# A mended order of seven products, one quarter read straight from its bank, and a re-dealt start and end around it, in a hybrid decoder layer

## The reference, cut to what matters

```python
h = rmsnorm(x, ln_pre)
z = h @ w_in        # columns: c_val, c_glu, c_gate, q, k, v, a_gate, g_conv, g_attn
u = c_val * sigmoid(c_glu)
c = causal_depthwise_conv(u, w_dw, taps=31) + b_dw
ya = (silu(layernorm(c)) @ w_pw * silu(c_gate)) @ w_br_conv
yb = (sliding_window_attention(rope(q), rope(k), v) * silu(a_gate)) @ w_br_attn
m = sigmoid(g_conv) * ya + sigmoid(g_attn) * yb
x = x + rmsnorm(m @ w_out, ln_post)
x = x + sigmoid(x @ w_ple_gate) * (p @ w_ple_proj)
```

## Time and profile before

| | us |
|---|---|
| median of 3 runs | 1156.72 (1155.39 to 1156.76) |
| the profiled execution | 1154.67 |
| its span | 1152.9 |
| PE busy, share of the span | 1109.1, 96% |
| DVE busy | 946.6, 82% |
| ACT, POOL busy | 482.8 (42%), 316.3 (27%) |
| granted clock of PE, mean | 0.988 |

### The profile page before, as it was taken

One profiled execution on the slowest core, in us unless ns is written; L12 is line 12 of the kernel. 1 busy time (PEld: TensorE's weight loads), 2 busy tenths in 40 slices (PEclk: granted clock), 3 DMA queues, 4 the chain that ended last, 5 costly groups with the idle time before them and its releaser, 6 DMA issues.

```text
span 1152.9 us, 16104 instructions
## 1 busy us (share of the span) xinstructions
PE 1109.1 (96%) x6040; PEld 898.0 (78%) x6040; DVE 946.6 (82%) x1092; ACT 482.8 (42%) x909; POOL 316.3 (27%) x218
## 2 busy tenths in 40 slices
PE   9799999999999949989999999999999999999998
PEld 8677777777777838867777788888888888888887
DVE  6998989989999996989888589769767968557776
ACT  6524343343433211157666443332536435444332
POOL 2067778787865941520000000000000000000000
PEclk9999999999999979999999999999999999999999
DMA  9802131221314213277871211236454653334555
GB/s 351 318 0 73 37 140 43 76 107 37 110 40 161 74 42 69 52 191 212 214 199 57 73 37 55 78 126 225 149 167 133 231 208 112 125 119 139 178 202 182
DMA packets 49540, 148.21 MB, mean 129 GB/s; under 512 B 5536, under 2 KB 6304, under 8 KB 47424
## 3 DMA queue, kind: packets, MB, share of 16 engines
q1 hardware_dynamic: 35648, 92.77, 23.9%
q10 hardware_dynamic: 11520, 37.75, 9.3%
q0 software_dynamic: 2304, 16.78, 6.0%
HBM read 119.37 MB, written 41.94 MB: 140 GB/s over the span
## 4 chain that ended last, share of the span: by engine, by line
PE 83%; DVE 8%; DMA 3%; ACT 2%; POOL 1%; issue 1%; SPq 1%; DVEq 0%; ACTq 0%; POOLq 0%
PE psg L740 35%; PE psg L927 23%; PE psb L1170 10%; PE psg L1078 6%; DVE last_sums L2037 3%; PE psb L992 1%; PE psg L1049 1%; PE psg L1170 1%; DMA conv<-xT 1%; DMA x_rows<-x_rows 1%; PE psg L793 1%; PE psg L1123 1%; PE psg L1010 1%; ACT kept L1434 1%; PE psg L1044 1%
## 5 line engine op out<-in xcount | busy, mean ns | idle before, releaser
L2037 DVE SCALAR_TENSOR_TENSOR psb<-conv,cols,psb 128x1021 f32<-128x1021 f32 (+6 forms) x196 | 232.9, 1265 | 0.0
L927 PE MATMUL psg<-early_hi,pair_w 128*128 128x512 f32 x448 | 139.4, 392 | 10.9 <-ACT kept L1434 10.9
L1229 POOL TENSOR_TENSOR pair_w<-early_raw,pair_w 128x512 fp32r<-128x512 f32 x91 | 125.2, 1381 | 62.0 <-ACT pair_w L1422 61.7
L740 PE MATMUL psg<-h_hi,w_hi 128*128 128x512 f32 x320 | 101.0, 397 | 23.5 <-POOL w_lo L1222 23.5
L927 PEld LDWEIGHTS psg<-early_hi,pair_w 128*128 128x128 f32 x448 | 83.0, 188 | 33.1 <-POOL pair_w L1229 15.2
L1212 POOL TENSOR_TENSOR rstd<-mean_sq,expo 128x4 f32<-128x4 f32 x3 | 3.1, 1021 | 381.0 <-DVE mean_sq L1874 363.4
L927 PE MATMUL psg<-h_hi,pair_w 128*128 128x512 f32 x336 | 103.5, 389 | 0.0
L1860 DVE TENSOR_TENSOR w_lo<-w_raw,w_hi 128x1024 fp32r<-128x1024 f32 x55 | 67.3, 1224 | 41.1 <-ACT w_hi L1335 40.8
L740 PE MATMUL psg<-h_hi,w_lo 128*128 128x512 f32 x320 | 99.5, 392 | 0.0
L740 PE MATMUL psg<-h_lo,w_hi 128*128 128x512 f32 x320 | 99.4, 392 | 0.0
L740 PEld LDWEIGHTS psg<-h_hi,w_hi 128*128 128x128 f32 x320 | 60.6, 191 | 37.5 <-issue 17.2
(11 more groups left out here) (338 smaller groups left out, 2598.7 us busy)
## 6 DMA issues: line engine op xcount, KB each, us to landing
w_raw<-weights SPq DMA_DIRECT2D x68, 512.0 KB, 3.4
gates<-ring ACTq DMA_DIRECT2D x24, 512.0 KB, 3.6
w_sums<-w_pairs POOLq DMA_DIRECT2D x12, 1024.0 KB, 7.8
ring<-gates ACTq DMA_DIRECT2D x24, 512.0 KB, 4.4
block_raw<-w_sums SPq DMA_DIRECT2D x32, 256.0 KB, 3.0
early_raw<-w_pairs SPq DMA_DIRECT2D x7, 1024.0 KB, 5.3
block_raw<-w_pairs SPq DMA_DIRECT2D x24, 256.0 KB, 3.6
early_raw<-w_pairs SPq DMA_DIRECT2D x7, 768.0 KB, 4.3
```

The lines of the kernel that those rows point to most:

```text
L740: mm = nc.tensor.matmul(psg[:, slot, h * HALF:(h + 1) * HALF], w[:, wslot, (wk + k) * P:(wk + k + 1) * P], r[:, k, h * HALF:(h + 1) * HALF ...
L927: mm = nc.tensor.matmul(bank, pair_w[:, at_w, w, k * P:(k + 1) * P], r[:, k, :], start=(not onto and k == 0 and m == 0), stop=(k == KP - 1 ...
L1229: nc.gpsimd.tensor_tensor(pair_w[:, at_w, 1, :], early_source(s, n), pair_w[:, at_w, 0, :].bitcast(F32), ALU.subtract).then_inc(early_spli ...
L2037: own.step(stt(dst, row[:, 0:S - shift], tap(shift), dst, ALU.mult, ALU.add))
```

## The change

The order of the seven products becomes P1, Q5, P6, P2, P7, Q3, P4. Quarter 1 is taken by DVE as kept Q5 minus P7's bank, so ACT's copy of P7 goes away, and P4 waits for that DVE operation. Around it: at the start the low halves of tiles 2 and 3 go from POOL to DVE and ACT's and DVE's operations there are re-ordered, `plain_input(0)` writes to `sums` and not to `conv`; the last part of the convolution uses PSUM like the others; DVE does two taps and not eleven before the stages and one more in each odd stage that is not VAL; after the stages ACT takes the sines after q tile 0, POOL does `low(Q0 + 2)` before it waits for them, and one `add_to_mean` moves back.

```diff
-ORDER = (P1, P2, Q5, P6, P7, Q3, P4)
+ORDER = (P1, Q5, P6, P2, P7, Q3, P4)
...
-            if q == KT - 1:
-                return last_sums[n][:]
             return psb[:, 2 * n:2 * n + 2, :].rearrange("p b s -> p (b s)")
...
-                if onto:
-                    pe.wait_ge(early_kept, kept_at(s, {P6: P1, P7: P6, Q3: Q5, P4: P7}[n]))
+                if n == P4:
+                    pe.wait_ge(early_read, early_read_by(s, 1))
+                elif onto:
+                    pe.wait_ge(early_kept, kept_at(s, {P6: P1, P7: P6, Q3: Q5}[n]))
...
-                    pe.wait_ge(conv_done, KT - 1)
+                    pe.wait_ge(conv_done, KT)
...
# POOL
-            nc.gpsimd.memset(sums[:], 0.0).then_inc(csum_done, 1)
...
             low(1)
-            low(2)
-            low(3)
             for s in range(len(EARLY)):
                 early_low(s, P1)
                 early_sum(s, Q5)
-                early_low(s, P2)
                 early_sum(s, P7)
                 early_low(s, Q5)
                 early_sum(s, P6)
+                early_low(s, P6)
+                early_low(s, P2)
                 early_sum(s, P4)
-                early_low(s, P6)
                 early_low(s, P7)
                 early_low(s, Q3)
                 early_low(s, P4)
+                if s == 3:
+                    pool.wait_ge(conv_done, 1)
+                    nc.gpsimd.memset(sums[:], 0.0).then_inc(csum_done, 1)
...
-            add_to_mean(4)
+            low(Q0 + 2)
             pool.wait_ge(sin_ready, 1)
...
-            for t in range(Q0 + 2, C0 - 1):
+            for t in range(Q0 + 3, C0 - 1):
                 low(t)
-            add_to_mean(5)
+                if t in (Q0 + 3, Q0 + 4):
+                    add_to_mean(t - Q0 + 1)
...
# ACT
+            high(0, 2)
+            product_done(0, 0)
+            nc.scalar.activation(tanh_t[:], psg[:, 0, :], ACT.Tanh, scale=0.5).then_inc(ps_free[0], 1)
             early_sum_high(1, 1)
+            high(0, 3)
             early_sum_high(2, 2)
-            product_done(0, 0)
-            high(0, 2)
-            nc.scalar.activation(tanh_t[:], psg[:, 0, :], ACT.Tanh, scale=0.5).then_inc(ps_free[0], 1)
-            high(0, 3)
             early_sum_high(0, 3)
...
-                if n in (P1, Q5, P6, P7):
+                if n in (P1, Q5, P6):
                     early_keep(s, n)
...
-                if j == 1:
+                if j == 0:
                     act.wait_ge(ang_ready, 1)
...
# DVE
+            early_row_sum(1, 0)
+            dve.wait_ge(w_lo_ready, PLE_STEPS + 2)
+            tile_low(2)
+            early_row_sum(2, 1)
+            early_row_sum(0, 2)
+            plain_input(0)
+            early_row_sum(3, 3)
+            tile_low(3)
             dve.wait_ge(tile_done, KT)
...
-                    a, b, op = ((early_bank(s, P2), kept[:, 0, :], ALU.add), (kept_q5[:], kept[:, 0, :], ALU.subtract),
+                    a, b, op = ((early_bank(s, P2), kept[:, 0, :], ALU.add), (kept_q5[:], early_bank(s, P7), ALU.subtract),
...
-            plain_input(0)
-            taps(11)
+            taps(2)
             plain_input(1)
             for s, (kind, i) in enumerate(EARLY):
                 for n in ORDER:
-                    if n == Q5:
-                        dve.wait_ge(early_made, 7 * s + PLACE[Q5] + 1)
+                    if n == P2:
                         early_take(s, 0)
+                    if n == P7:
+                        early_take(s, 1)
                     if n == Q3:
-                        early_take(s, 1)
                         early_take(s, 2)
                     if n == P4 and kind == VAL:
                         early_take(s, 3)
-                    if n == Q5:
+                    if n == P2:
                         taps(1 if kind == VAL else 2)
                     elif n == Q3:
-                        taps(0 if kind == VAL else 1)
+                        taps(0 if kind == VAL else 1 + s % 2)
                     else:
                         taps(2)
...
-            taps(26)
+            taps(TAPS * KT)
```

More of the change, by code:

```diff
@@ L156, in build @@
         early_rest = at("early_rest", [HALF], F32, GB + 14 * KB)
-        last_sums = [at(f"last_sums{n}", [S], F32, GB + KB * (28 + 4 * n) - 192) for n in range(2)]
         v_last = at("v_last", [P], F32, GB + 24 * KB - 192)
@@ L540, in kept_at @@
         def kept_at(s, n):
-            return 4 * s + {P1: 1, Q5: 2, P6: 3, P7: 4}[n]
+            return 3 * s + {P1: 1, Q5: 2, P6: 3}[n]
         def early_read_by(s, n):
@@ L1428, in early_keep @@
                     act.wait_ge(ps_free[1], K_TILE // 2 + 4)
[L1429 to L1430 removed]
                 elif s > 0:
[L1432 to L1433 removed]
+                    act.wait_ge(early_read, early_read_by(s - 1, {P1: 0, Q5: 1, P6: 2}[n]))
+                dst = {P1: kept[:, 0, :], P6: kept[:, 1, :], Q5: kept_q5[:]}[n]
                 nc.scalar.activation(dst, early_bank(s, n), ACT.Copy).then_inc(early_kept, 1)
@@ L1997, in early_row_low, with plain_input @@
                 nc.vector.tensor_tensor(early_lo[:, n], sum_of(n), early_hi[:, n].bitcast(F32), ALU.subtract).then_inc(early_s_ready, 1)
-            for made, n in enumerate((1, 2, 0, 3)):
-                early_row_sum(n, made)
+            def plain_input(q):
+                product_done(q, 1)
+                dve.wait_ge(ps_free[0], KT // 2 + q + 1)
+                if q == 1:
+                    dve.wait_ge(early_s_ready, 4)
+                into = sums[:] if q == 0 else conv[:, CONV_ROWS[q], :]
+                stt(into, tanh_t[:], 1.0, psg[:, 1, :], ALU.add, ALU.mult).then_inc(ps_free[1], 1)
+            early_row_sum(1, 0)
[6 more added lines that the diff above has]
+            tile_low(3)
             dve.wait_ge(tile_done, KT)
@@ L2003, in _ @@
                 early_row_low(n, made + 1)
-            def plain_input(q):
-                product_done(q, 1)
-                dve.wait_ge(ps_free[0], KT // 2 + q + 1)
-                dve.wait_ge(early_s_ready, 4)
-                stt(conv[:, CONV_ROWS[q], :], tanh_t[:], 1.0, psg[:, 1, :], ALU.add, ALU.mult).then_inc(ps_free[1], 1)
             def conv_steps():
@@ L2018, in tap @@
                         return cols[:, COL_TAPS + i * TAPS + PAD - shift:COL_TAPS + i * TAPS + PAD - shift + 1]
-                    row = conv[:, i, :]
-                    sums_of = (conv_sums(q, 0), conv_sums(q, 1))
+                    out = conv[:, i, :]
+                    row = sums[:] if q == 0 else out
+                    sums_of = (conv_sums(0), conv_sums(1))
                     if q < 2:
@@ L2039, in conv_steps @@
                     own.wait()
-                    own.step(nc.vector.tensor_scalar(row[:, 0:1], row[:, 0:1], tap(0), col("b_dw", i), ALU.mult, ALU.add))
-                    own.step(stt(row[:, 1:], row[:, 1:], tap(0), sums_of[1][:, 1:], ALU.mult, ALU.add))
+                    own.step(nc.vector.tensor_scalar(out[:, 0:1], row[:, 0:1], tap(0), col("b_dw", i), ALU.mult, ALU.add))
+                    own.step(stt(out[:, 1:], row[:, 1:], tap(0), sums_of[1][:, 1:], ALU.mult, ALU.add))
                     yield
                     own.wait()
-                    nc.vector.tensor_tensor(row[:, 2:], row[:, 2:], sums_of[0][:, 2:], ALU.add).then_inc(conv_done, 1)
+                    nc.vector.tensor_tensor(out[:, 2:], out[:, 2:], sums_of[0][:, 2:], ALU.add).then_inc(conv_done, 1)
                     yield
@@ L2237, in _ @@
                     tile_low(C0 + p // 2 + 1)
-                if p > 1 and p % 2 == 0:
-                    taps(2)
                 if p == 4:
@@ L2248, in _ @@
                 if p == 14:
-                    taps(TAPS)
                     dve.wait_ge(sums_hi_ready, 1)
```

8 lines of the change are left out of this document (3 added, 5 removed).

## The result

The changed kernel took 1108.23 us, the median of four runs (1107.42 to 1108.64); the kernel before, on the same chip, 1156.74 (1155.39 to 1158.41). The ratio is 0.9579, with a 95% interval of 0.9562 to 0.9596: 48.5 us less. The forecast was 45.5 less, at 1111.2, and its range of 1107.5 to 1120 held the time, 0.7 us from its lower end. The profiled execution of the changed kernel took 1108.18 us, its span 1106.4, with PE's granted clock at 1.00 (before 0.988).

What follows compares the result with a forecast made beforehand. PE (96% busy) was taken as the bound through its stops, with DVE second and the later date at the scores deciding. 9.3 + 14.8 + 21.4 = 45.5 us off 1156.72 gave 1111.2 us, range 1107.5 to 1120.

Steps and rivals of the forecast that it cites:

- Start, 9.3 us: Before the stages: no PE stop at tile 2 and a better clock, P1 at 73.6 instead of 82.9.
- Stages, 14.8 us: In the 14 stages: the 1.06 us stop between P6 and P7 goes from each, 14.8 us in all.
- P4's wait: Rival, in each stage: P4 waiting behind DVE's list replaces the copy, slower than before; 1.4 us of slack; chance 0.04.
- Quarter 1, 0.65 us less of DVE a stage: In each stage: taking it with one operand in PSUM costs DVE 0.69 us, not 1.34.
- After the stages, 21.4 us: From the stages' end to the first score: 110.3 us instead of 131.7, long stop and pause gone.
- PE's date: At the first score: stages end at 340.2, plus 109.7 us of PE's work, gives 449.9.
- handover of 0.6 us: At the scores: 0.6 us added to 109.7 us of PE work because DVE and PE meet nearly together.
- Its landing: Ahead of the scores: SP's last of six small transfers lands in 2.3 to 5.30 us, at 447.5 to 452.5.
- The last part in PSUM: Convolution's last part, after the stages: 26 taps at 1.20 us, 31.2 us; DVE gains 16 us.
- Beyond the scores nothing is moved: From the first score to the end: no change, 0 us, PE already full.
- DVE as the bound at the scores: Rival, at the scores: dates 0 to 2.6 us apart, DVE's slips land whole, 1115 to 1118; chance 0.15.
- The long stop moved one tile on: Rival, after the stages: stop recurs if the sines run after q tile 1 once more, 1116; chance 0.06.

Runs made afterwards that it cites:

- two kernels on the start: Against the changed kernel: low halves of tiles 2 and 3 back on POOL, 1109.83 us; ACT's high part of tile 2 behind two sums again, 1114.68 us.
- ACT's order: Changed kernel with ACT's high part of tile 2 behind two sums again, DVE's low half behind two row sums: 1114.68 us.
- stage part: Kernel before with only the new product order, quarter 1 read directly from P7's bank and P4's new wait: 1142.86 us.
- late sines: Changed kernel with the sines after q tile 1 again, POOL's order kept new: 1115.06 us.
- two more taps a stage: Changed kernel with two taps moved ahead of quarter 1 in each stage: 1121.59 us, median of three runs.
- fewer taps: Changed kernel with one tap less in each of the four odd stages that are not VAL, four more behind the stages: 1115.73 us.
- later additions: Changed kernel with P7 copied by ACT again and POOL's four stage additions one stage on, behind the stage's last sum: 1116.09 us.
- copied quarter: Changed kernel with P7 copied by ACT again and quarter 1 taken from the two copies, new order kept: 1119.66 us.
- SBUF sums: Changed kernel with the last part's two accumulators back in SBUF: 1122.62 us.
- moved addition: Changed kernel with four taps moved behind the stages and one POOL addition moved behind the four transfers that followed it: 1121.13 us.
- old angles: Changed kernel with the sines after q tile 1 and q tile 2's low half behind POOL's wait for them again: 1126.56 us.
- one tap moved: Changed kernel with one tap moved in each stage from behind P4 to ahead of quarter 1: 1109.61 us.

## Why the prediction was right

Point by point, by its own steps.

- **Start, 9.3 us.** 8.6 came. Tile 2 begins with no stop and the clock is 1.00, so of these 9.4 us were had (23.60 + 7.52 before, 21.76 after); but everything ahead of tile 2 was 0.8 us later than before (52.56 instead of 51.8), which was taken as unchanged. That is within what executions with one and the same start differ by. DVE's first low half ended at 51.3, 1.2 us ahead of PE, as forecast. The two kernels on the start show that the early high part is what lets PE go on; of the stop's 7.5 us, ACT's order alone brings back 4.3.
- **Stages, 14.8 us.** Exactly so, in the trace and, alone on the kernel before, by 14.0 us. P4's wait has the room of 1.4 us that was worked out, and no wait for POOL's new order is left.
- **Quarter 1, 0.65 us less of DVE a stage.** Right as a duration (0.68 against 1.31) and too small as the worth of the step. Its bound was "0.65 us in the seven tightest stages, 4 us", for a direct read that is slow all the same, which no run made; copying again, which the prediction did not price, costs 11.4. What it left out is the place of the copy in ACT's list behind a wait for POOL, and what DVE's lateness draws after it at the scores.
- **After the stages, 21.4 us.** 22.0 came. PE's date was given as 449.9 and was 450.58, all of it from the late start. The stop after q tile 1 is gone; POOL's three operations took 5.9 us and not 7.6, so q tile 3's low had 6 us to spare and not 4.6. The handover of 0.6 us did not happen: the unpacking landed some 2.4 us early, after a `rope(1)` from 437.5 to 442.5, which the prediction put at 436.9 to 442. Its landing was given as 2.3 to 5.3 us, and it took 2.3; here the prediction was lucky, for it had no term for what decides between them. POOL's first 1 MB transfer was issued at 448.05, 2.4 us behind SP's last small one; the runs in which it came among the six had 5.2 to 7.6.
- **The last part in PSUM.** Priced at 16 us of DVE's time, with PE's date deciding; putting it back costs 14.4. The size is near, but of those, 3.7 us are a stop of PE for a low half that POOL could not finish, which no step had.
- **"Beyond the scores nothing is moved."** Wrong by 1.1 us, in the good direction: POOL's addition and `vstep` no longer meet.
- **Rivals.** DVE as the bound at the scores: its date and PE's lay some 2.4 us apart, within the 0 to 2.6 of the prediction; four more taps were enough to make it the bound. The long stop moved one tile on: shown by the late sines, at the place forecast. P4's wait: shown with two more taps a stage.

Undone one by one, the direct read, the last part, the angles and the two halves of the start cost 11.4 + 14.4 + 18.3 + 1.6 + 6.4 = 52.1 us; with the stage part's 14.0 that is more than the 48.5 that all bring together. The reason is the meeting of two dates. That a part that helps DVE is worth little while PE still stops is argued: no run had such a part alone on the kernel before. Shown is that once PE has no stop, whatever makes DVE over 2 us late costs its own length, a meeting with POOL, often a slow landing, and a pause, with a clock of 0.89 to 0.94 over the 30 us from the first score. How much of the 7.5 us of the fewer taps each of these three is, apart from the 4.8 us to the scores, was not separated: the rest is 2.7, of which the slow gate half is 2.0.

## What to carry to other kernels

Where two engines meet, work out both dates, and treat the smaller margin, here 2 us, as the price list for every edit on either: inside it an edit is free, beyond it it costs more than its length. A short operation is as late as what stands ahead of it in its engine's list, so ask what the list waits for before pricing a copy at its own duration. And an operation moved out of the way also releases what stood behind it: look at which transfers start earlier, and what they will meet.

## What the runs showed of the hardware

- One GpSimd instruction (128x1024, two SBUF inputs) took 12.38 us instead of 2.41 while VectorE ran nine instructions with two SBUF inputs one after the other, each in 1.24 or 1.25 us and 1.17 us apart. The blocking isn't bounded by one instruction of the other side.
- The same VectorE subtraction of 128x512 took 0.68 us with one operand in PSUM, whether GpSimd worked beside it or not. With both in SBUF it took 0.683 at best (in the run with the later additions) and 1.31 at the median of either run that copies, with GpSimd at work beside it. The slower place was not PSUM.
- A small transfer of SyncE (64 KB) is slow when a 1 MB transfer of GpSimd was issued just ahead of it. In six kernels one came among the six small ones, and the last of these landed in 5.24, 5.30, 5.54 and 5.62 us where it came 0.9 us before it (the later additions, the kernel before, the copied quarter, the stage part alone), in 6.52 where it came 1.1 (the SBUF sums) and in 7.61 where it came 1.3 (the moved addition). It landed in 2.3 us in the eight others, in which no large one came just ahead of it. That is a pattern in order; no run moved the large transfer alone.
- In the seven kernels with a PE pause at the scores, of 3.8 to 8.2 us, the granted clock was 0.89 to 0.94 over the 30 us from the first score, and 1.00 in the changed kernel. The pause's length does not order them: 0.94 with 3.8, 4.0 and 4.3 us, 0.90 with 4.1, 0.89 with 5.1, 0.92 with 7.2, 0.91 with 8.2. At 0.90 and 0.89 the 24 matmuls of the first gate half took 7.6 and 7.7 us instead of 5.7. Four kernels without that pause, whose PE stopped 1.8 to 2.3 us once in the attention (late sines, old angles, ACT's order, one tap moved), had 0.94 to 0.95 in the same stretch.
